# A hybrid decoder layer: loads, weight splits and row norms at the start of both feed-forward layers, rearranged

## The chip, the cores and the metric

The kernel runs on one core of a Trainium2 chip. The metric is the device time in microseconds of one execution, the median of the runs shown. TensorE multiplies matrices, VectorE and ScalarE work on elements, POOL (GpSimd) does further element work, and SP issues the transfers (DMA). Every engine has a queue of its own and takes its instructions in order; semaphores order the engines among each other.

## The reference

One layer for 64 sample rows and 1,024 prompt rows (T = 1,088 columns, with 1,024 features in KT = 8 tiles of 128 partitions). The parts around the change:

```python
def rmsnorm(x, g):
    y = xf * lax.rsqrt(jnp.mean(xf * xf, axis=-1, keepdims=True) + EPS)
    return (y * g).astype(x.dtype)
def swiglu(x, w_gate, w_up, w_down):
    return (jax.nn.silu(x @ w_gate) * (x @ w_up)) @ w_down
x = x + 0.5 * swiglu(rmsnorm(x, p['g_ffn1']), p['w1_gate'], p['w1_up'], p['w1_down'])
...                                   # mixer, output projection, cross attention
x = x + 0.5 * swiglu(rmsnorm(x, p['g_ffn2']), p['w2_gate'], p['w2_up'], p['w2_down'])
```

The hidden width is 2,816, 22 tiles of 128.

## The kernel before

Every matrix product of fp32 operands is made of three products of a rounded high part and a rest, the low part (L807 hi x hi, L808 lo x hi, L809 hi x lo). ScalarE or POOL writes high parts by a copy to fp32r, VectorE or POOL low parts by a subtraction. The 1,088 columns stand in three chunks, CH = 288, 512 and 288 columns.

A feed-forward layer has an opening and a steady part. The opening (`conventional` on TensorE, `ffn_layer` on ScalarE and VectorE) computes the first two hidden tiles in the plain way: gate 0 and up 0 for each chunk, then gate 1 for the three chunks, then up 1. The weights of tile 0 are split by POOL (`split_first`), those of tile 1 by ScalarE and VectorE (`conv_hi`, `conv_lo`). The gain g multiplies x before these products (it is part of the high and low parts), and the factor 1/rms of each column, `rstd`, multiplies the gate result (`gate_first`), before SiLU, and the up result (`ffn_up`).

The norm: the squares of x are added over the eight tiles to `acc` (128 partitions x 1,088). A product of `acc` with a 128x128 matrix of ones (`sum_chunk`, L835) puts the column sum of each chunk in all partitions; VectorE scales it to `rstd` (`mean_squares`, L1960), ScalarE takes the root (`rms`, L1460), VectorE the reciprocal (`inverse_rms`, L1968), each on 128 partitions x the chunk. The final norm of the kernel does it in another way: `acc` is the stationary operand and one column of ones the moving one (L985), so the sums stand as columns of 96 or 128 partitions; root (L1922) and reciprocal (L2749) work on these few columns, and a product with the identity (L998) spreads them to a row in all partitions.

The steady part computes the other twenty hidden tiles in quads, a block scheme with seven products in place of eight (`quad`; products 1 to 7 are j = 0 to 6 there, 24 matmuls x 2 of 272 columns each). It needs x times the gain (`gained`, L1497, ScalarE in place), sums and differences of quarter blocks of x (`moving_sum`, L2029, VectorE, four of them), and their high and low parts (`moving_hi`, L1501, ScalarE; `moving_lo`, L2037, VectorE), and the same of the weights (`quad_hi`, L1513; `quad_lo`, L2058). VectorE takes results out (`quad_part`, L2085; C11, C22, C21 and C12 are its four blocks), `keep_p1` (L1528, ScalarE) and `keep_u2` (L2106, VectorE) keep intermediate ones. In TensorE's `quad`, product 3 waits for `keep_p1`, product 5 for `keep_u2` and product 7 for the eviction of C22.

The order within each engine's queue is written out by hand. In the first opening ScalarE's queue is: high parts of x, high part of the gate 1 weights, 24 squares, three roots, high part of up 1, then for each chunk two tiles of `gained` and the SiLU of the chunk, two more tiles of `gained`, high parts of the block sums. VectorE's: low parts of x, sums of squares with the gate results of tile 0 copied out between, low part of gate 1, three `mean_squares`, for each chunk reciprocal and `gate_first`, low part of up 1, `ffn_up` of chunk 0, the first block sums (they wait for four `gained` tiles), `ffn_up` of chunk 1, the second and third block sums (they wait for all eight), `ffn_up` of chunk 2, and the operands of the first quad. In the second opening the squares are made in the projection before it.

Of the kernel before, what the change touches and what calls it, by code (L numbers as in the profile page):

```python
# [22 lines left out]
F32 = mybir.dt.float32  # L23
F32R = mybir.dt.float32r
ALU = mybir.AluOpType
# [96 lines left out]

SUM_BANK, RSTD_BANK, LAST_BANKS = 5, 2, DOWN_BANKS[:6]
# [70 lines left out]
def build(nc, t_in, t_out):  # L194
    ctx = ExitStack()
    with ctx:
# [32 lines left out]
        small = at("small", [P, NSM], C0 + 1440)  # L229

# [165 lines left out]
        x_in = [sem(f"x_in{c}") for c in range(NC)]  # L396
        ones_set = sem("ones_set")
# [9 lines left out]
        F_TOTAL = dict(gu_in=32, gu1_in=32, raw_in0=16 * (FI - 1), raw_in1=16 * (FI - 1), cv_a=4, cv_hi=2, cv_lo=2,  # L407
# [79 lines left out]

        y_done, y_tab, eps_set, row_mm = sem("y_done"), sem("y_tab"), sem("eps_set"), sem("row_mm")
# [14 lines left out]
        def _(sp):  # L503
            def load_first(f, w, m, done):
                for i in range(2):
                    sp.dma_start(raw_gu[i][:, m, :, :], w[i, :, m, :, :]).then_inc(f[done], 16)
# [176 lines left out]
            load_first(f, t_in["w_gu2"], 0, "gu_in")  # L683
            load_first(f, t_in["w_gu2"], 1, "gu1_in")
# [15 lines left out]
        def _(pool):  # L700
# [10 lines left out]
            def split_first(f):  # L711

                one = ones[:, :].unsqueeze(1).to_broadcast([P, KT, P])
                pool.wait_ge(f["gu_in"], upto(f, "gu_in", 32))
                steps = Steps(pool, f["cv_a"], upto(f, "cv_a", 0))
                for i, k in enumerate(("gate0", "up0")):
                    steps.done(pool.tensor_tensor(c_hi[k][:, :, :], raw_gu[i][:, 0, :, :], one, ALU.mult))
                    steps.done(pool.tensor_tensor(c_lo[k][:, :, :], raw_gu[i][:, 0, :, :],
                                                  c_hi[k][:, :, :].bitcast(F32), ALU.subtract))
# [81 lines left out]
        def _(pe):  # L801
# [35 lines left out]

            def conv_gate(f, t, c, feed=None):
# [11 lines left out]
            def conventional(f, feed, before, after):  # L850
# [10 lines left out]
                for c in range(NC):  # L861
                    conv_gate(f, 1, c)
# [2032 lines left out]
```

## Time and profile before

| | us |
|---|---|
| median of 3 runs | 2226.09 (2224.31 to 2226.76) |
| the profiled execution, its own time | 2230.03 |
| its span, first to last instruction | 2228.1 |
| TensorE busy | 2166.5 |
| VectorE busy | 1345.7 |
| ScalarE busy | 712.0 |
| POOL busy | 399.7 |

The busy times are those of one profiled execution; matmuls overlap, and a busy TensorE is not one at its peak. The granted clock of TensorE has two levels, 1.0 (2.4 GHz) and 0.5 (1.2 GHz), and was 0.991 on average. The first feed-forward opening lies at the start of the span, to about 103 us, the second from about 1462 to 1547 us.

### The profile page before, as it was taken

The numbers are of one execution on the slowest core, as the hardware profiler recorded it, in microseconds if no ns is written. First come the engines' busy times: TensorE is split into PE (matmuls) and PEld (weight loads), VectorE is DVE, ScalarE is ACT, GpSimd is POOL, SyncE is SP. The second block draws the span as 40 slices with busy tenths as digits, with TensorE's granted clock in tenths as the row PEclk, the third lists the DMA queues.
The fourth block names the chain that finished last, engine by engine and source line by source line (L and its number), as shares of the span: only waits on it lengthen the run. The fifth ranks groups of instructions, "written<-read, shape, count | busy, mean of one in ns | idle before, by whom it ended". The sixth has DMA issues, their size and how long they took to land. (4 is left out here: it accounts for less than half of the span.)

```text
span 2228.1 us, 37795 instructions
## 1 busy us (share of the span) xinstructions
PE 2166.5 (97%) x15020; PEld 2016.9 (91%) x15020; DVE 1345.7 (60%) x2013; ACT 712.0 (32%) x1270; POOL 399.7 (18%) x427
## 2 busy tenths in 40 slices
PE   6899999999999999989999999999999999999998
PEld 5899999998989888878898887989999999989897
DVE  7966766664423678899526155368766766644234
ACT  6422322322212325547403034154223223222122
POOL 1000000000000256768535321520000000000003
PEclk9999999999999999999999999999999999999999
DMA  3212212116423221153411062312122122164222
GB/s 139 77 59 96 76 58 96 67 59 236 125 67 93 73 96 39 59 143 103 163 38 58 20 246 77 135 40 78 59 96 76 58 96 76 59 232 125 66 72 81
DMA packets 70864, 206.67 MB, mean 93 GB/s; under 512 B 9703, under 2 KB 31207, under 8 KB 63079
## 3 DMA queue, kind: packets, MB, share of 16 engines
q1 hardware_dynamic: 67808, 201.84, 26.7%
q10 hardware_dynamic: 2951, 3.35, 0.4%
q8 instruction: 76, 1.25, 0.2%
q14 instruction: 29, 0.24, 0.0%
HBM read 161.14 MB, written 41.23 MB: 91 GB/s over the span
## 5 line engine op out<-in xcount | busy, mean ns | idle before, releaser
L807 PE MATMUL ps<-act_hi,op_hi 128*128 128x272 f32 x1280 | 370.2, 289 | 10.2 <-ACT p L1528 9.6
L808 PE MATMUL ps<-act_lo,op_hi 128*128 128x272 f32 x1280 | 371.6, 290 | 0.0
L809 PE MATMUL ps<-act_hi,op_lo 128*128 128x272 f32 x1280 | 370.8, 290 | 0.0
L707 POOL TENSOR_TENSOR w_hi<-w_raw,ones 128x256 fp32r<-128x256 f32 x148 | 134.4, 908 | 1033.3 <-DMA w_raw<-in_w_plain 790.6
L807 PE MATMUL ps<-act_hi,w_hi 128*128 128x288 f32 (+1 forms) x864 | 290.4, 336 | 7.3 <-DVE act_lo L1981 2.0
L807 PE MATMUL ps<-hs_hi,dn_hi 128*128 128x288 f32 (+1 forms) x864 | 284.9, 330 | 1.3 <-DVE x L2161 1.1
L809 PE MATMUL ps<-act_hi,w_lo 128*128 128x288 f32 (+1 forms) x864 | 283.9, 329 | 0.0
L808 PE MATMUL ps<-hs_lo,dn_hi 128*128 128x288 f32 (+1 forms) x864 | 282.4, 327 | 0.0
L809 PE MATMUL ps<-hs_hi,dn_lo 128*128 128x288 f32 (+1 forms) x864 | 282.3, 327 | 0.0
L807 PE MATMUL ps<-t_hi,op_hi 128*128 128x272 f32 x960 | 277.2, 289 | 0.2 <-DVE hid_t L2002 0.2
L808 PE MATMUL ps<-t_lo,op_hi 128*128 128x272 f32 x960 | 277.1, 289 | 0.0
L809 PE MATMUL ps<-t_hi,op_lo 128*128 128x272 f32 x960 | 277.1, 289 | 0.0
L808 PE MATMUL ps<-act_lo,w_hi 128*128 128x288 f32 (+1 forms) x792 | 259.6, 328 | 0.0
L807 PEld LDWEIGHTS ps<-act_hi,op_hi 128*128 128x128 f32 x1280 | 243.3, 190 | 11.1 <-issue 10.5
L808 PEld LDWEIGHTS ps<-act_lo,op_hi 128*128 128x128 f32 x1280 | 243.0, 190 | 0.0
L809 PEld LDWEIGHTS ps<-act_hi,op_lo 128*128 128x128 f32 x1280 | 243.0, 190 | 0.0
L1513 ACT ACTIVATE op_hi<-sums 128x512 fp32r<-128x512 f32 x160 | 101.2, 632 | 382.6 <-DVE sums L2066 208.2
L807 PEld LDWEIGHTS ps<-act_hi,w_hi 128*128 128x128 f32 x864 | 162.8, 188 | 25.7 <-issue 8.0
L807 PEld LDWEIGHTS ps<-t_hi,op_hi 128*128 128x128 f32 x960 | 181.2, 189 | 0.4 <-issue 0.4
L809 PEld LDWEIGHTS ps<-t_hi,op_lo 128*128 128x128 f32 x960 | 181.2, 189 | 0.0
L808 PEld LDWEIGHTS ps<-t_lo,op_hi 128*128 128x128 f32 x960 | 180.7, 188 | 0.0
L807 PEld LDWEIGHTS ps<-hs_hi,dn_hi 128*128 128x128 f32 x864 | 162.0, 188 | 17.9 <-DVE x L2161 3.4
(332 smaller groups left out, 4215.1 us busy)
## 6 DMA issues: line engine op xcount, KB each, us to landing
raw_gu<-in_w_gu SPq DMA_DIRECT2D x40, 1024.0 KB, 5.1
w_raw<-in_w_plain SPq DMA_DIRECT2D x54, 512.0 KB, 3.6
dn_raw<-in_w_dn SPq DMA_DIRECT2D x44, 512.0 KB, 4.2
hid<-hid_o SPq DMA_DIRECT2D x40, 544.0 KB, 3.7
hr<-hid SPq DMA_DIRECT2D x88, 144.0 KB, 2.1
hr<-hid SPq DMA_DIRECT2D x44, 256.0 KB, 2.7
x<-x_keep SPq DMA_DIRECT2D x16, 544.0 KB, 5.1
ck_T<-in_ck SPq DMA_DIRECT2D x8, 1024.0 KB, 7.2
```

Of the source, the lines that this page charges most:

```text
L707: steps.done(pool.tensor_tensor(hi[:, r, :], raw[:, r, :], one, ALU.mult))
L807: pe.matmul(out, wh, ah, start=(first and n == 0), stop=False, skip_group_check=goes_on)
L808: pe.matmul(out, wh, al, start=False, stop=False, skip_group_check=goes_on)
L809: ins = pe.matmul(out, wl, ah, start=False, stop=end, skip_group_check=goes_on)
L1513: act.activation(op_hi[j][:, :, :], src, ACT.Copy).then_inc(f["w_hi"], 1)
```

## The change

It rearranges both openings. Loads: in the first opening the gate 0 weights come ahead of x, x's first chunk is loaded in two halves, the up 0 weights behind it. An activation on one element right after the constants loads ScalarE's table; ScalarE makes the high part of gate 0 there, and POOL splits in pieces of two tiles of 128 columns (SHORT = 2). Norms: `sum_chunk`, `mean_squares`, `rms` and `inverse_rms` give way to `sum_columns`, `roots`, `inverse_columns`, `row` and `take_row`, in the way of the final norm, in both openings. Order: `normed(1)` and `normed(2)` (the wait for a row and `gate_first`) stand behind the first block sums and behind `ffn_up` of chunk 1; `keep_p1` stands ahead of operands 5 and 6 (j = 4 and 5) on ScalarE; the fourth block sums stand behind `keep_u2` on VectorE, and operand 6 (j = 5) ahead of the low parts of these sums. The identity is loaded once more for each opening. The core of the diff:

```diff
+COL_BANK, ROW_BANKS = 6, (7, 6, 7)
+        n_id = at("n_id", [P, P], C0 + 1440)
 # sync
+            load_first(f, t_in["w_gu1"], 0, 0, "gt_in")
             for c, (o, n) in enumerate(CH):
                 if c == 0:
-                    load_first(f, t_in["w_gu1"], 0, "gu_in")
-                sp.dma_start(x[:, :, o:o + n], t_in["x"][:, :, o:o + n]).then_inc(x_in[c], 16)
-            load_first(f, t_in["w_gu1"], 1, "gu1_in")
+                    sp.dma_start(x[:, 0:KH, o:o + n], t_in["x"][:, 0:KH, o:o + n]).then_inc(x_half_in, 16)
+                    sp.dma_start(x[:, KH:KT, o:o + n], t_in["x"][:, KH:KT, o:o + n]).then_inc(x_in[c], 16)
+                    load_first(f, t_in["w_gu1"], 1, 0, "gu_in")
+                else:
+                    sp.dma_start(x[:, :, o:o + n], t_in["x"][:, :, o:o + n]).then_inc(x_in[c], 16)
+            for i in range(2):
+                load_first(f, t_in["w_gu1"], i, 1, "gu1_in")
+            sp.dma_start(n_id[:, :], t_in["ident"]).then_inc(n_tab, 16)
 # gpsimd, split_first: pieces of SHORT tiles; the high part of the first gate 0 is left to ScalarE
+                        for r in rows:
+                            ins = pool.tensor_tensor(c_hi[k][:, r, :], raw_gu[i][:, 0, r, :], one, ALU.mult)
 # tensor
+            def sum_columns(key, c, adds):
+                w, at_ = WIDTH[c], CH[c][0]
+                pe.wait_ge(sq_used, SQ0[key] + adds)
+                if c and key == "ffn1":
+                    pe.wait_ge(rms_done, SUM0[key] + c)
+                for k in range(COLUMNS[c]):
+                    i = sum(COLUMNS[:c]) + k
+                    ins = pe.matmul(ps[0:w, COL_BANK, i:i + 1], acc[:, at_ + k * w:at_ + (k + 1) * w], ones[:, 0:1],
+                                    start=True, stop=True)
+                ins.then_inc(ssq_mm, 1)
+            def row(f, key, c):
+                w = WIDTH[c]
+                pe.wait_ge(rstd_done, SUM0[key] + c + 1)
...
+                for k in range(COLUMNS[c]):
+                    ins = pe.matmul(ps[:, ROW_BANKS[c], k * w:(k + 1) * w],
+                                    rms_col[c][0:w, k:k + 1].to_broadcast([w, P]), n_id[0:w, 0:w],
+                                    start=True, stop=True)
+                ins.then_inc(row_mm, 1)
+            def norm_ffn1(i):          # i = 0..2 behind up 0 of chunk i, 3..5 behind gate 1 of chunk i - 3
+                if i == 1:
+                    sum_columns("ffn1", 0, KT)
+                if i == 2:
+                    row(ffn["ffn1"], "ffn1", 0)
+                    sum_columns("ffn1", 1, 2 * KT)
+                if i == NC:
+                    sum_columns("ffn1", 2, 3 * KT)
+                if i > NC:
+                    row(ffn["ffn1"], "ffn1", i - NC)
+            def norm_ffn2(i):
+                if i == 0:
+                    for c in range(NC):
+                        sum_columns("ffn2", c, 2 * KT)
+                if i == 1:
+                    row(ffn["ffn2"], "ffn2", 0)
+                    row(ffn["ffn2"], "ffn2", 1)
+                if i == 2:
+                    row(ffn["ffn2"], "ffn2", 2)
 # scalar
+            def roots(key, which):
+                for c in which:
+                    w, k, i = WIDTH[c], COLUMNS[c], sum(COLUMNS[:c])
+                    act.wait_ge(ssq_mm, SUM0[key] + (c + 1 if key == "ffn1" else NC))
+                    act.activation(rms_col[c][0:w, 0:k], ps[0:w, COL_BANK, i:i + k], ACT.Sqrt, bias=eps[0:w, :],
+                                   scale=1.0 / D).then_inc(rms_done, 1)
+            def take_row(f, key, c):
+                o, n = CH[c]
+                act.wait_ge(row_mm, f["n"] * NC + c + 1)
+                act.activation(rstd[:, o:o + n], ps[:, ROW_BANKS[c], 0:n], ACT.Copy).then_inc(ssq_ev, 1)
                 conv_hi(f, "up1")
+                if key == "ffn1":
+                    roots(key, [2])
+                else:
+                    take_row(f, key, 0)
+                    take_row(f, key, 1)
                 for c in range(NC):
                     gained(f, gain, range(2 * c, 2 * c + 2))
+                    if c and (c == 2 or key == "ffn1"):
+                        take_row(f, key, c)
                     silu(f, 0, c)
                 gained(f, gain, range(2 * NC, KT))
...
+                keep_p1(f, Quad(0))
                 for j in range(4, 6):
                     quad_hi(f, Quad(0), 0, j)
-                keep_p1(f, Quad(0))
...
+            act.activation(act_hi[:, 0, 0:1], c_("g_ffn1", 0), ACT.Copy, scale=c_("g_ffn1", 0)).then_inc(table_set, 1)
+            act.wait_ge(ffn["ffn1"]["gt_in"], 16)
+            act.activation(c_hi["gate0"][:, :, :], raw_gu[0][:, 0, :, :], ACT.Copy).then_inc(ffn["ffn1"]["cv_a"], 1)
...
-            for c in range(NC):
-                chunk_squares(c)
-            rms("ffn1")
+            chunk_squares(0)
+            chunk_squares(1)
+            roots("ffn1", [0])
+            chunk_squares(2)
+            take_row(ffn["ffn1"], "ffn1", 0)
+            roots("ffn1", [1])
 # vector
+            def inverse_columns(key, which):
+                for c in which:
+                    w, k = WIDTH[c], COLUMNS[c]
+                    dve.wait_ge(rms_done, SUM0[key] + c + 1)
+                    dve.reciprocal(rms_col[c][0:w, 0:k], rms_col[c][0:w, 0:k]).then_inc(rstd_done, 1)
             def ffn_layer(f, key):
-                for c in range(NC):
-                    inverse_rms(key, then=lambda c: gate_first(f, c), which=[c])
+                def normed(c):
+                    dve.wait_ge(ssq_ev, SUM0[key] + c + 1)
+                    gate_first(f, c)
+                normed(0)
                 conv_lo(f, "up1")
+                if key == "ffn1":
+                    inverse_columns(key, [2])
                 ffn_up(f, 0, 0)
                 dve.wait_ge(f["xg"], upto(f, "xg", KH))
                 moving_sum(f, 0, 0, 0, TH, 0, 0)
+                normed(1)
                 ffn_up(f, 0, 1)
+                normed(2)
                 dve.wait_ge(f["xg"], upto(f, "xg", KT))
...
+                moving_lo(f, 4, lambda a: act_hi[:, a:a + 2, TH:T], lambda a: act_lo[:, a:a + 2, TH:T], 0, TH)
+                quad_lo(f, Quad(0), 0, 4)
+                keep_u2(f, Quad(0))
                 dve.wait_ge(f["t_sum"], upto(f, "t_sum", 6))
                 moving_sum(f, 0, 0, KH, 0, KH, TH)
-                moving_lo(f, 4, ...)
-                quad_lo(f, Quad(0), 0, 4)
-                keep_u2(f, Quad(0))
+                quad_lo(f, Quad(0), 0, 5)
                 dve.wait_ge(f["t_sum"], upto(f, "t_sum", 8))
                 moving_lo(f, 6, lambda a: t4_hi[:, a:a + 2, :], lambda a: t4_lo[:, a:a + 2, :], 0, 0)
-                quad_lo(f, Quad(0), 0, 5)
-            mean_squares("ffn1", D, which=[0, 1])
-            mean_squares("ffn1", D, which=[2])
+            inverse_columns("ffn1", [1])
```

## Rows read from the trace of the kernel before

**Rows 1.** The page's part 1: busy us (share of the span) xinstructions of each engine.

```profile
PE 2166.5 (97%) x15020; PEld 2016.9 (91%) x15020; DVE 1345.7 (60%) x2013; ACT 712.0 (32%) x1270; POOL 399.7 (18%) x427
```

**Rows 2.** TensorE's list of waits, 0 to 110 us: us in total, times, longest.

```profile
PE ps L807 <- ACT p L1528: 6.1, 1, 6.1
```

**Rows 3.** TensorE's list of waits, 1460 to 1560 us.

```profile
PE ps L807 <- ACT p L1528: 3.6, 1, 3.6
...
PE ps L807 <- DVE sg L2085: 0.3, 1, 0.3
```

**Rows 4.** The chain of waits in the second opening: start us, us, what.

```profile
1488.96 0.48 PE ps L835 x2
...
1493.05 1.96 DVE rstd L1968
...
1495.40 3.36 DVE rstd L1968
...
1507.47 4.89 DVE x L2029 x4
...
1543.36 0.74 DVE sg L2085
```

**Rows 5.** TensorE's timeline in the first opening: start us, us, instruction.

```profile
47.55 0.29 PE L808 MATMUL ps<-act_lo,c_hi_gate 128*128 128x288 f32 x1
47.68 0.29 PE L809 MATMUL ps<-act_hi,c_lo_gate 128*128 128x288 f32 x1
...
99.54 0.36 PE L807 MATMUL ps<-act_hi,op_hi 128*128 128x272 f32 x1
```

**Rows 6.** Timeline of ScalarE, POOL and VectorE at the start; in brackets idle before, releaser.

```profile
11.08 1.28 ACT L1469 ACT_TABLE_LOAD   x1 [11.08 <-DMA x<-in_x]
...
12.82 2.35 POOL L717 TENSOR_TENSOR c_hi_up<-raw_gu,ones 128x1024 fp32r<-128x1024 f32 x1
...
13.01 16.32 DVE L1981 SCALAR_TENSOR_TENSOR act_lo<-x,cst,act_hi 128x288 fp32r<-128x288 f32 x24 [12.00 <-ACT act_hi L1469]
```

**Rows 7.** VectorE's timeline in the first opening.

```profile
45.13 1.22 DVE L2023 TENSOR_TENSOR c_lo_gate<-raw_gu,c_hi_gate 128x1024 fp32r<-128x1024 f32 x1
...
54.10 0.69 DVE L2017 TENSOR_TENSOR gate_t<-gate_t,rstd 128x512 f32<-128x512 f32 x1
...
59.06 2.48 DVE L2029 TENSOR_TENSOR x<-x 128x1088 f32<-128x1088 f32 x2
...
62.79 4.89 DVE L2029 TENSOR_TENSOR x<-x 128x1088 f32<-128x1088 f32 x4
```

**Rows 8.** ScalarE's timeline in the first opening.

```profile
49.41 2.28 ACT L1497 ACTIVATE x<-x,cst 128x1088 f32<-128x1088 f32 x2
...
55.55 0.62 ACT L1487 ACTIVATE gate_t<-gate_t 128x512 f32<-128x512 f32 x1
...
85.22 2.11 ACT L1501 ACTIVATE t_hi<-x 128x1088 fp32r<-128x1088 f32 x2 [0.74 <-DVE x L2029]
...
91.26 0.63 ACT L1513 ACTIVATE op_hi<-sums 128x512 fp32r<-128x512 f32 x1 [3.92 <-DVE t_lo L2037]
```

**Rows 9.** ScalarE's timeline in the second opening.

```profile
1491.27 2.28 ACT L1497 ACTIVATE x<-x,cst 128x1088 f32<-128x1088 f32 x2
```

**Rows 10.** TensorE by line and shape in the final norm: xcount, us in all, mean ns, idle.

```profile
L998 PE MATMUL ps<-y_id,lrup 128*128 128x128 f32 x8 | 1.1, 275 | 0.0
L985 PE MATMUL ps<-ones,acc 128*128 128x1 f32 x8 | 0.9, 239 | 0.0
```

**Rows 11.** Instructions of lines 1922 and 2749: duration ns min/median/max, first and last start.

```profile
L1922 ACT ACTIVATE lrup<-ps,lrup x3: 246/258/259, 2188.7 to 2218.5; 96x3 f32<-96x3 f32 x2, 128x4 f32<-128x4 f32 x1
...
L2749 DVE RECIPROCAL lrup<-lrup x3: 160/172/178, 2189.0 to 2220.1; 96x3 f32<-96x3 f32 x2, 128x4 f32<-128x4 f32 x1
```

**Rows 12.** Stretches of 2 us: busy us of each engine, granted clock, DMA share, GB/s.

```profile
80.00:82.00 2.00, 0.00 (x0) 0.00 (x0) 1.97 (x4) 0.00 (x0) 0.00 (x0) 0.63 0.00 0
...
90.00:92.00 2.00, 2.00 (x15) 2.00 (x15) 1.90 (x4) 0.74 (x2) 0.00 (x0) 0.81 0.00 0
```

More of the change, by code:

```diff
@@ L229, in build @@
         small = at("small", [P, NSM], C0 + 1440)
+        assert P <= 144
+        n_id = at("n_id", [P, P], C0 + 1440)
         ACC0 = P0 + 68608
@@ L503, in _, with load_first @@
         def _(sp):
-            def load_first(f, w, m, done):
-                for i in range(2):
-                    sp.dma_start(raw_gu[i][:, m, :, :], w[i, :, m, :, :]).then_inc(f[done], 16)
+            def load_first(f, w, i, m, done):
+                sp.dma_start(raw_gu[i][:, m, :, :], w[i, :, m, :, :]).then_inc(f[done], 16)
             def load_quad(f, w, q, s):
@@ L682, in _ @@
             sp.wait_ge(stored, 16 * 9)
-            load_first(f, t_in["w_gu2"], 0, "gu_in")
-            load_first(f, t_in["w_gu2"], 1, "gu1_in")
+            sp.dma_start(n_id[:, :], t_in["ident"]).then_inc(n_tab, 16)
+            load_first(f, t_in["w_gu2"], 0, 0, "gt_in")
+            load_first(f, t_in["w_gu2"], 1, 0, "gu_in")
+            for i in range(2):
+                load_first(f, t_in["w_gu2"], i, 1, "gu1_in")
             for m in range(KT):
@@ L711, in split_first @@
             def split_first(f):
-                one = ones[:, :].unsqueeze(1).to_broadcast([P, KT, P])
-                pool.wait_ge(f["gu_in"], upto(f, "gu_in", 32))
+                one = ones[:, :].unsqueeze(1).to_broadcast([P, SHORT, P])
                 steps = Steps(pool, f["cv_a"], upto(f, "cv_a", 0))
[L716 to L719, printed above, removed]
+                for i, (k, loaded) in enumerate((("gate0", "gt_in"), ("up0", "gu_in"))):
+                    pool.wait_ge(f[loaded], upto(f, loaded, 16))
+                    rows = [slice(r, r + SHORT) for r in range(0, KT, SHORT)]
+                    if f["n"] == 0 and k == "gate0":
+                        steps.n = 1
+                        pool.wait_ge(f["cv_a"], 1)
+                    else:
+                        for r in rows:
+                            ins = pool.tensor_tensor(c_hi[k][:, r, :], raw_gu[i][:, 0, r, :], one, ALU.mult)
+                        steps.done(ins)
+                    for r in rows:
+                        ins = pool.tensor_tensor(c_lo[k][:, r, :], raw_gu[i][:, 0, r, :],
+                                                 c_hi[k][:, r, :].bitcast(F32), ALU.subtract)
+                    steps.done(ins)
             def split_plain(s, p, hi=w_hi, lo=w_lo, less=0, both=True):
@@ L862, in conventional @@
                     conv_gate(f, 1, c)
+                    after(NC + c)
                 pe.wait_ge(f["cv_lo"], upto(f, "cv_lo", 2))
@@ L1913, in _ @@
             conv_hi(ffn["ffn2"], "gate1")
-            rms("ffn2")
+            roots("ffn2", range(NC))
             act.wait_ge(act_lo_done, SPLIT0["ffn2"] + NC * KT)
-            ffn_layer(ffn["ffn2"], "g_ffn2", 16 + 16 * KT)
+            ffn_layer(ffn["ffn2"], "ffn2", "g_ffn2", 16 + 16 * KT)
             def final_sqrt(c):
                 w, k = WIDTH[c], COLUMNS[c]
-                act.wait_ge(eps_set, 1)
+                act.wait_ge(eps_set, 2)
                 act.wait_ge(ssq_mm, SUM0["final"] + c + 1)
@@ L2275, in _ @@
             dve.memset(ones[:, :], 1.0).then_inc(ones_set, 1)
+            dve.memset(eps, EPS).then_inc(eps_set, 1)
             dve.wait_ge(cst_in, 16)
@@ L2729, in _ @@
             lo_parts("co", lambda k: xq[:, k, :])
-            plain_residual("co", PAIR_CO, "ffn2", "g_ffn2", lambda s: None,
-                           lambda: mean_squares("ffn2", D, which=[0, 1]))
-            mean_squares("ffn2", D, which=[2])
+            plain_residual("co", PAIR_CO, "ffn2", "g_ffn2", lambda s: None, lambda: None)
             conv_lo(ffn["ffn2"], "gate1")
+            inverse_columns("ffn2", range(NC))
             for c in range(NC):
```

39 lines of the change are left out of this document (24 added, 15 removed).

## The prediction

> **What bounds the kernel now.** Part 1 of the page comes first: TensorE is busy in 97% of the span, so a change of order can only win from its few idle places [rows 1]. The list of TensorE's waits gives those of the two feed-forward openings: 6.1 us in the first and 3.6 us in the second for `p`, the copy of the first block product (it releases the third of the seven products of the first quad) and, in the second, 0.3 us for `sg` [rows 2, 3]. The 0.3 us is the row that matters. `sg` at L2085 is VectorE's second eviction (C22), for which the seventh product waits. In the second opening that product begins as soon as this eviction ends, 1543.36 + 0.74 = 1544.1, start 1544.23. In the first it begins at 99.54 [rows 5]; VectorE's queue there ends the same eviction at 99.4. So the seventh product starts when VectorE lets it, and the waits for `p` before it cost nothing: what TensorE would save there it would wait for `sg` later. The chain of waits says so for the second opening: TensorE up to the third sum at 1488.96, then VectorE from the reciprocals at 1493.05 to `sg` [rows 4]. After the seventh product TensorE has no wait of note until the down products, so a shift of its start is the change of the time.
>
> **What goes.** Three reciprocals of whole rows (1.96, 3.36 and 1.96 us [rows 4]) and three takes of sums leave VectorE; on 96 or 128 columns a root costs 0.26 us and a reciprocal 0.17 [rows 11]. What comes instead is work on TensorE (columns and rows, 0.11 us each by [rows 10]: about 0.5 us + 0.7 us for a chunk of 288, 0.9 + 0.9 for the one of 512, against 1.8 us for the three old sums, so some 2 us more in each layer) and three takes on ScalarE. That TensorE work is hidden while `sg` decides; without that cover it would cost 2 us twice.
>
> **What VectorE waits for next.** It needs the scaled x (`gained`, ScalarE) before its second block sums, which began at 62.79 and 1507.47 [rows 7, 4]. Before, ScalarE scaled all eight tiles without waiting for VectorE's first block sums: from 49.41, the first opening needed 13.4 us to 62.79, the second 16.2 from 1491.27 [rows 8, 9]. Now `normed(1)` stands behind the first block sums in VectorE's queue, SiLU of chunk 1 stands before tiles 4 and 5 in ScalarE's, and `take_row` 2 and `normed(2)` stand before the SiLU that holds tiles 6 and 7. The two engines take turns. Behind each waiting SiLU in ScalarE's queue stand the next scalings, and VectorE's second block sums wait for those. From the first scaling: unchanged 6.2 us to the end of tile 3 (two pairs of 2.28, a table load of 1.28, a SiLU [rows 8, 6]), then the first block sums 2.5 [rows 7], normed(1) 0.6, SiLU 0.6, a pair 2.2, take 0.4, normed(2) 0.45, SiLU 0.4, the last pair 2.2, and some eight hand-overs of 0.05 to 0.1: 15.9 us. Durations of the row takes are those of ScalarE's 288 and 512 column operations [rows 8].
>
> **When the first scaling starts.** *Second opening.* Columns in place of two sums, +0.4 on 1488.96; rows 0 and 1, 1.6; take of row 1, 0.7: 1491.7, against 1491.27. With 15.9 the second block sums start at 1507.6, +0.1. *First opening.* VectorE's 24 low parts ran from 13.01 to 29.33, two of them held behind POOL's long splits for about 2 us each [rows 6]. Half of x and an early table load let them start near 8.6, when x has landed to the half (x's first chunk landed at 11.08 as the third load after the constants; now it is half of it as the second). But the splits of POOL are now twelve pieces instead of four, each with about 0.6 us (a quarter of 2.35) in which a low part can stand, and ScalarE's last high part is bound by x's landing as before; I take an end at 26.4 (25.1 to 27.0), 2.9 earlier. A table load and a root now stand between the second and third chunk of squares, +1.0. So the low part of the next weights, before 45.13 + 1.22 [rows 7], ends at 44.4. Then on the new path: the first gate product, 24 steps of 0.133 = 3.2 [rows 5], columns of chunk 2 0.6, the root 0.26, three hand-overs: scaling starts at 48.8, 0.6 earlier than before, because `roots(2)` stands in front of it. With 15.9: 64.7, +1.9. Bounds: VectorE's end at 25.1 with no loss at the table load gives 46.5 and -0.4; TensorE late by its start at the lower clock gives up to +3.4.
>
> **The tail.** The fourth block sums move behind `keep_u2`. ScalarE's high parts of them (1.1 us a half [rows 8]) now lie open before VectorE's low parts, with one operand's low part of 0.7 as cover: +0.7. And ScalarE's operand 7 waits for those low parts (the 3.92 us wait of [rows 8] is that wait); operand 6, which filled VectorE meanwhile, is already done: +0.8. Together +1.5 in each opening. `keep_p1` one place earlier lets products 3 to 5 run sooner, which is worth nothing while `sg` decides. So `sg`, and with it the seventh product, shifts by +1.9 + 1.5 = +3.4 (1.1 to 4.9) and by +0.1 + 1.5 = +1.6 (1.2 to 2.1).
>
> **What costs nothing.** The identity's load stands behind the first opening's weights and ahead of the second's; row 0 stands behind 144 products of the first two weight blocks, 19 us and more at 0.133 [rows 5], and the next loads in SP's queue, the quads' weights, wait for the low parts at 44 as they did at 46 [rows 7]. POOL's sixteen pieces in the second opening stand under the last product of the stage before; they would have to take twice their time (0.6 us of work each, a quarter of 2.35 [rows 6]) to delay the first gate product, and what they held back would be VectorE's low parts, 0.6 us each. The final norm only counts its rows from another base.
>
> **The clock.** TensorE runs products 3 to 6 sooner and then stands still until `sg`: in the first opening product 6 can end near 97.0 and 7 starts near 102.9, in the second 1540.8 and 1545.8, so 5 to 6 us idle. In the trace the granted clock fell to 0.5 (the 1.2 GHz level) in the 6.1 us stop at product 3 and stayed there until 90.8, 6.1 us after the restart at 84.6 [rows 2, 12]. Before, that cost nothing, since `sg` came later. Now the lower level would fall on product 7 and those after it, where TensorE is the path. Bounds: 0 if the clock holds, 3.0 for a whole 6.1 us at half; I take 2.3, nearer to the row of a stop of this length, and less than all of it, since the lower level may begin before the restart.
>
> **The sum.** 3.4 + 2.3 + 1.6 + 2.3 = +9.6 us. The profiled execution took 2230.03 us around a span of 2228.1; +9.6 makes 2239.6. It stood 3.9 above the median of the runs, 2226.09, so the median should be 2235.7. What a measurement of this kernel can tell from no change is about 0.2%, 4.5 us.
>
> **Rivals.** *The clock holds.* Everything as above without 2.3 twice: 2231.1. For it: the idle time stands between products, and the level also depends on what ran before; against it the stop named. Half of this case lies over 0.2%. *VectorE's shorter queue decides.* If ScalarE's scalings come before VectorE needs them, VectorE's saved 7.3 + 1.4 us and its head start carry through: `sg` 11.0 - 1.5 = 9.5 us sooner in the first opening; in the second TensorE's own products, 3 us later by the new matmuls, allow 3.5 of it. About 2213, faster. It decides from the point where the second scaling pair ends before 55.6 and SiLU 1 no longer waits for normed(1). For it: VectorE is the chain in [rows 4] and the reciprocals are 7.3 us of it. Against it: the queue order, by which scaling waits three times for VectorE. The Trainium skill (Perfetto Trace Analysis, Optimizing Scalar/DVE Operations) says that with a saturated VectorE it may pay to give work to ScalarE. By that rule the time would come out as in this rival, 2213; the trace agrees on the saturation, and no run here yet shows the order of turns. *Nothing to be seen.* The first opening's head start is larger than I take (scaling from 46.5) and the clock costs little: +1.1 + 1.2 + about 1, 2229.
>
> **How the numbers follow.** Forecast with clock loss 0.57, all of it over 0.2% slower. Clock holds 0.13, divided evenly between slower and same. Nothing to be seen 0.12, same. Faster 0.18. That makes slower 0.64, same 0.18, faster 0.18. Likeliest 2235.7, its own range 2231 to 2239.2 (4.9 + 3.0 + 2.1 + 3.0 = 13.0 at the top). The range of 8 in 10 reaches down through the case of no change to 2224.5; below that lies most of the faster rival, above 2239.2 about 0.05.
>
> **What would show it.** Right: in TensorE's list of waits the waits for `p` are gone and waits of 4 to 6 us for `sg` L2085 stand in their place; ScalarE shows waits for VectorE's `gate_t` and takes between the scaling pairs; the second block sums start near 64.7 and 0 to 1 us late in the second opening; VectorE shows waits for ScalarE of 1 to 4 us; the granted clock is 0.5 around product 7. Wrong: VectorE reaches the second block sums before 62 and 1507, or product 7 starts before 99 and 1544; or the turns are as I say but the clock stays at 1.0.

## The result and the profile after

The changed kernel took 2240.40 us in the median of 6 runs (2233.41 to 2242.98), the kernel before 2226.43 (6 runs, 2224.31 to 2228.82): ratio 1.0058, 95% interval 1.0046 to 1.0070. Run again beside some of the experiments it took 2237.1 (6 runs), ratio 1.0047 (1.0030 to 1.0064). All twelve together have their median at 2239.05. So the change is slower, as forecast, by 14.0 us in the first six runs and 10.8 in the second six, where 9.6 were forecast; the first median lies 1.2 us above the range's upper end of 2239.2, the second inside the range. The profiled execution took 2242.98 us around a span of 2240.9, 12.8 more than the span before.

Part 1 of the profile's page says that TensorE stayed the engine that is busiest by far; its 13.7 us more than in [rows 1] are about the whole loss, though the change gives it only 68 more instructions:

```profile
PE 2180.2 (97%) x15088; PEld 2031.6 (91%) x15088; DVE 1331.4 (59%) x2008; ACT 714.4 (32%) x1278; POOL 403.1 (18%) x447
```

From TensorE's list of waits, first opening (0 to 140 us) and, behind the second dots, second opening (1460 to 1600 us): us in total, times, longest.

```profile
...
PE ps L829 <- DVE sg L2190: 3.4, 1, 3.4
PE ps L829 <- DVE c_lo_gate L2128: 3.3, 1, 3.3
PE ps L829 <- DVE t_lo L2142: 3.0, 1, 3.0
...
PE ps L829 <- DVE sg L2190: 4.9, 1, 4.9
PE ps L868 <- DVE acc L2050: 1.1, 1, 1.1
```

The waits for `p` of [rows 2, 3] are gone, and in each opening a wait for `sg`, VectorE's second eviction, stands where before there was 0.3 us or none. New is the 3.3 us wait for `c_lo_gate`, the low part of the second weight block. TensorE's timeline at both places (start us, us, instruction, in brackets idle before and releaser):

```profile
43.38 0.61 PE L829 MATMUL ps<-act_hi,c_hi_gate 128*128 128x288 f32 x1 [3.28 <-DVE c_lo_gate L2128]
43.78 0.44 PE L830 MATMUL ps<-act_lo,c_hi_gate 128*128 128x288 f32 x1
44.02 0.44 PE L831 MATMUL ps<-act_hi,c_lo_gate 128*128 128x288 f32 x1
...
95.57 0.36 PE L829 MATMUL ps<-t_hi,op_hi 128*128 128x272 f32 x1 [2.96 <-DVE t_lo L2142]
103.74 0.57 PE L829 MATMUL ps<-act_hi,op_hi 128*128 128x272 f32 x1 [3.40 <-DVE sg L2190]
...
1554.86 0.56 PE L829 MATMUL ps<-act_hi,op_hi 128*128 128x272 f32 x1 [4.92 <-DVE sg L2190]
```

The seventh product starts at 103.74 instead of 99.54 [rows 5], +4.2, and in the second opening at 1554.86 instead of 1544.23. The steps of the gate product lie 0.24 us apart (43.78, 44.02), not 0.133 as in [rows 5]. The stretches of 2 us say why (start and end, length, busy us of TensorE, its weight loads, VectorE, ScalarE and POOL, each with its number of instructions; granted clock; DMA share; GB/s):

```profile
42.00:44.00 2.00, 0.62 (x2) 0.63 (x3) 2.00 (x5) 0.34 (x1) 0.00 (x0) 0.50 0.00 0
44.00:46.00 2.00, 2.00 (x10) 2.00 (x10) 1.25 (x2) 0.00 (x0) 0.00 (x0) 0.50 0.82 229
...
104.00:106.00 2.00, 2.00 (x10) 2.00 (x10) 1.97 (x4) 0.98 (x2) 0.00 (x0) 0.50 0.00 0
...
1486.00:1488.00 2.00, 2.00 (x7) 1.61 (x7) 1.95 (x5) 1.98 (x4) 0.00 (x0) 0.50 0.05 12
...
1556.00:1558.00 2.00, 2.00 (x11) 2.00 (x11) 2.00 (x5) 1.82 (x3) 0.00 (x0) 0.50 0.00 0
```

At all four places the granted clock is 0.5, the 1.2 GHz level, just where TensorE has work that others wait for.

VectorE's timeline of the first opening, to be held against [rows 7]:

```profile
42.11 1.22 DVE L2128 TENSOR_TENSOR c_lo_gate<-raw_gu,c_hi_gate 128x1024 fp32r<-128x1024 f32 x1
...
50.05 0.17 DVE L2077 RECIPROCAL lrup<-lrup 96x3 f32<-96x3 f32 x1 [4.80 <-ACT lrup L1534]
54.07 0.46 DVE L2107 TENSOR_TENSOR hid_t<-ps,gate_t 128x288 f32<-128x288 f32 x1 [3.84 <-ACT gate_t L1568]
...
56.19 2.49 DVE L2134 TENSOR_TENSOR x<-x 128x1088 f32<-128x1088 f32 x2 [1.17 <-ACT x L1578]
...
62.46 0.46 DVE L2122 TENSOR_TENSOR gate_t<-gate_t,rstd 128x288 f32<-128x288 f32 x1 [1.00 <-ACT rstd L1541]
65.62 4.90 DVE L2134 TENSOR_TENSOR x<-x 128x1088 f32<-128x1088 f32 x4 [2.70 <-ACT x L1578]
```

And ScalarE's, against [rows 8]:

```profile
49.76 0.26 ACT L1534 ACTIVATE lrup<-ps,lrup 96x3 f32<-96x3 f32 x1 [7.42 <-PE ps L868]
49.92 2.29 ACT L1578 ACTIVATE x<-x,cst 128x1088 f32<-128x1088 f32 x2
...
59.32 0.63 ACT L1568 ACTIVATE gate_t<-gate_t 128x512 f32<-128x512 f32 x1 [2.43 <-DVE gate_t L2122]
59.85 2.28 ACT L1578 ACTIVATE x<-x,cst 128x1088 f32<-128x1088 f32 x2
...
62.95 0.44 ACT L1568 ACTIVATE gate_t<-gate_t 128x288 f32<-128x288 f32 x1 [0.53 <-DVE gate_t L2122]
63.30 2.29 ACT L1578 ACTIVATE x<-x,cst 128x1088 f32<-128x1088 f32 x2
```

This is the late start and the taking of turns: VectorE's low part comes 3.0 us sooner than before, then VectorE waits 4.80 us for the root of chunk 2 and 3.84, 1.17, 0.77 (not shown), 1.00 and 2.70 us for other work of ScalarE, 14.3 in all, and ScalarE 7.42 us for TensorE's column sums and 2.43 and 0.53 us for VectorE. Its first scaling starts at 49.92 (49.41 before), and VectorE's second block sums at 65.62 (62.79), 15.7 us behind it. In the second opening the place to count from is VectorE's last addition of squares, here first in the kernel before and then in the changed one:

```profile
1474.70 1.36 DVE L1952 TENSOR_TENSOR acc<-acc,sq 128x544 f32<-128x544 f32 x2 [0.78 <-DVE x L2616]
```

```profile
1482.57 1.36 DVE L2050 TENSOR_TENSOR acc<-acc,sq 128x544 f32<-128x544 f32 x2 [0.78 <-DVE x L2730]
...
1501.04 2.29 ACT L1578 ACTIVATE x<-x,cst 128x1088 f32<-128x1088 f32 x2
...
1516.74 4.90 DVE L2134 TENSOR_TENSOR x<-x 128x1088 f32<-128x1088 f32 x4 [2.70 <-ACT x L1578]
```

So the profiled kernel enters the second opening 7.9 us late, its block sums are 9.3 us late and its seventh product 10.6. The 12.8 us of span are then 4.2 to the seventh product, 3.7 more up to the second opening, 2.8 within it, and 2.1 behind its seventh product. In the profile of the second six runs (span 2238.6) the same four parts are 3.7, 0.3, 2.8 and 3.7: the parts within the openings come again, nearly, those between and behind them do not.

In the second opening the first scaling comes 18.5 us behind the last addition of squares (1482.57 to 1501.04), before 16.6 (1474.70 to 1491.27 [rows 9]). TensorE's products there, first before, from the first gate product of the second chunk to the old third sum, then in the changed kernel, column sums and rows:

```profile
1477.16 0.80 PE L807 MATMUL ps<-act_hi,c_hi_gate 128*128 128x512 f32 x1
...
1488.80 0.65 PE L835 MATMUL ps<-acc,ones 128*128 128x288 f32 x2
```

```profile
1483.98 2.20 PE L868 MATMUL ps<-ones,acc 128*96 128x1 f32 x20 [1.05 <-DVE acc L2050]
1486.05 0.78 PE L829 MATMUL ps<-act_hi,c_hi_gate 128*128 128x512 f32 x1
...
1498.79 1.72 PE L883 MATMUL ps<-n_id,lrup 96*128 96x96 f32 x14
```

The 48 products of that chunk took 12.7 us instead of 11.6, at first at the lower clock, and the twenty column products 2.1 instead of 1.3 for the three old sums (1476.12 to 1477.16 and 1488.80 to 1489.06).

### The profile page after: what moved, and what is told of

Same layout as the page of the kernel before. It is cut to its first block and busy times, and to the rows that moved or that the text cites. A ratio compares the mean times of both kernels' runs of the same rounds, so it can differ in the third digit from the quotient of the medians.

```text
span 2240.9 us, 37971 instructions
## 1 busy us (share of the span) xinstructions
PE 2180.2 (97%) x15088; PEld 2031.6 (91%) x15088; DVE 1331.4 (59%) x2008; ACT 714.4 (32%) x1278; POOL 403.1 (18%) x447
## 5 line engine op out<-in xcount | busy, mean ns | idle before, releaser
L829 PEld LDWEIGHTS ps<-act_hi,op_hi 128*128 128x128 f32 x1280 | 243.0, 190 | 10.5 <-issue 8.7
L829 PEld LDWEIGHTS ps<-hs_hi,dn_hi 128*128 128x128 f32 x864 | 162.0, 188 | 18.6 <-DVE x L2266 3.5
```

Source lines behind the costliest of these rows:

```text
L829: pe.matmul(out, wh, ah, start=(first and n == 0), stop=False, skip_group_check=goes_on)
```

## The experiments

Medians are in us, each beside the kernel before on the same chip (2226.2 to 2227.2). The fourth and fifth columns are from the one profiled execution of each, which can lie some us above the median (loads_alone: 5.5): start of the seventh product in the first opening, and its distance from VectorE's second block sums. "Lower clock" is the mean over the runs of span times (1 - mean granted clock), the time that the lower level can have cost TensorE at most. It also counts the lower level where TensorE waits or is not the path: in the profile before, 17.1 us at that level (80.5 to 90.8 and 1527.8 to 1534.6) end before the seventh products, whose start VectorE sets.

| kernel | median | ratio (95%) | 7th product | distance | lower clock |
|---|---|---|---|---|---|
| before (beside the first four) | 2226.21 | 1 | 99.54 | 36.75 | 18.0 |
| changed | 2240.40 | 1.0058 (1.0046-1.0070) | 103.74 | 38.12 | 24.6 |
| changed, again | 2237.10 | 1.0047 (1.0030-1.0064) | 103.25 | 38.10 | 23.1 |
| tail_back | 2233.15 | 1.0030 (1.0019-1.0041) | 99.90 | 36.77 | 21.8 |
| columns_sooner | 2237.83 | 1.0048 (1.0034-1.0062) | 101.47 | 38.12 | 25.0 |
| no_turns | 2235.79 | 1.0039 (1.0026-1.0052) | 100.92 | 41.78 | 23.7 |
| product_twice | 2231.38 | 1.0021 (1.0012-1.0030) | 102.93 | 38.10 | 18.6 |
| loads_alone | 2222.44 | 0.9984 (0.9976-0.9993) | 96.31 | 36.77 | 20.0 |
| columns_alone | 2237.83 | 1.0046 (1.0031-1.0061) | 103.46 | 36.76 | 21.0 |
| copy_alone | 2228.98 | 1.0006 (0.9997-1.0014) | 99.01 | 36.78 | 18.0 |
| tail_alone | 2234.64 | 1.0031 (1.0018-1.0044) | 100.46 | 38.10 | 20.3 |
| woven | 2221.41 | 0.9982 (0.9973-0.9991) | 92.31 | 36.77 | 18.8 |
| woven_filled | 2220.31 | 0.9967 (0.9957-0.9978) | 92.47 | 36.79 | 18.3 |

The theory: the loss is a later seventh product, by the turns and by the tail, and the lower clock behind it. The rivals: the turns or the tail are hidden by VectorE's own work; or it is the loads; or the clock falls where it likes and the stops have nothing to do with it.

**The changed kernel again,** as it was:

> The changed kernel once more, as the measure for the others of this call. If the median of 2240.4 us is the kernel's own, it comes again within 1.5 us. If part of it was where the clock happened to fall in the stages between the two openings (24 us at the lower level in the changed kernel's profile against 17 us before), it comes out near 2237 and the profile shows 17 us there.

It came out at 2237.1, as in the second case, and its profile has 17 us at the lower level between the openings, not 24. Half of that difference is 3.4 us, about what the median fell by. That the one made the other is not shown: the two sets of six runs overlap (2233.41 to 2242.98 and 2233.71 to 2244.05), and the execution with 17 us itself took 2240.54.

**The tail back** (changed kernel, VectorE's queue):

```diff
+ moving_sum(f, 0, 0, KH, 0, KH, TH)      # with its two waits
  moving_lo(f, 4, ...); quad_lo(f, Quad(0), 0, 4); keep_u2(f, Quad(0))
- moving_sum(f, 0, 0, KH, 0, KH, TH)
- quad_lo(f, Quad(0), 0, 5)
  moving_lo(f, 6, ...)
+ quad_lo(f, Quad(0), 0, 5)
```

> The changed kernel with VectorE's tail in the order of before (fourth block sums ahead of the low parts of the fourth operand, low part 5 behind those of t4); everything else as changed. If the tail costs what the prediction said (1.5 us an opening), the distance from VectorE's second block sums to the start of the seventh product goes back from 38.1 us (103.74 - 65.62 and 1554.86 - 1516.74) to 36.75 as before (99.54 - 62.79), and the median from 2240.4 to about 2237.5. Rival: the new order of the tail is hidden, and the loss is the turns and the clock alone: both distances stay at 38.1 and the median at 2240.4.

The distance went back to 36.77 as expected, 1.35 us in each opening, but the median fell by 5.9 us from the twelve runs' 2239.05 (3.8 to 6.2 by the ratios), not by 2.9. TensorE's stops show where more can come from. In the changed kernel it stopped for `t_lo` and again for `sg`, and the clock was at 0.5 behind the second stop. Here (the seventh product, then stretches of 2 us) the clock fell in an earlier stop and was back before the seventh product:

```profile
99.90 0.36 PE L829 MATMUL ps<-act_hi,op_hi 128*128 128x272 f32 x1 [1.85 <-DVE sg L2190]
```

```profile
90.00:92.00 2.00, 2.00 (x11) 2.00 (x10) 2.00 (x3) 0.39 (x1) 0.00 (x0) 0.50 0.00 0
...
100.00:102.00 2.00, 2.00 (x17) 2.00 (x18) 1.97 (x4) 0.83 (x2) 0.00 (x0) 1.00 0.03 8
```

Part of the difference, 49.92 to 47.43 us at the first scaling, is not the tail's, which comes later: in this execution TensorE stopped only 0.5 us for the low part and kept its clock. In the second opening the clock fell behind the seventh product here too, for 3.4 us where the changed kernel had 6.8.

**The column sums sooner** (TensorE's queue, first norm):

```diff
  sum_columns("ffn1", 1, 2 * KT)
+ sum_columns("ffn1", 2, 3 * KT)
- if i == NC:
-     sum_columns("ffn1", 2, 3 * KT)
```

> The changed kernel with the column sums of chunk 2 of the first norm ahead of the second weight block's first gate product instead of behind it: they run in TensorE's stop from 40.0 to 43.4. By the reading that the scaling starts late because its queue holds the root of chunk 2, the first scaling goes from 49.92 to about 42.6 us. The second block sums then wait for the row of chunk 1, which stands behind the second gate product: from 65.6 to 60.6 if TensorE keeps its full clock there (63.2 if it falls as now), so 2 to 5 us off the median, 2235.4 to 2238. Rival: VectorE's own queue is the limit from 42 us on, and the scaling's start is worth nothing: second block sums stay at 65.6, median 2240.4.

ScalarE's timeline has the first scaling where it was expected, 7.6 us sooner, and the wait that takes its place:

```profile
42.34 2.28 ACT L1577 ACTIVATE x<-x,cst 128x1088 f32<-128x1088 f32 x2
...
55.70 0.60 ACT L1540 ACTIVATE rstd<-ps 128x512 f32<-128x512 f32 x1 [7.13 <-PE ps L883]
```

The next turn, the row of chunk 1, stands behind the second gate product, so the second block sums came at 63.35 and the seventh product 2.3 us sooner. The median is at the upper end of the expectation; against the changed kernel's second median (2237.1) it is no gain. The late start was real, but only one of a series of waits.

**Without the turns:**

```diff
  # ScalarE
- gained 0-1, silu 0, gained 2-3, take_row 1, silu 1, gained 4-5, take_row 2, silu 2, gained 6-7
+ gained 0-1, silu 0, gained 2-7, take_row 1, silu 1, take_row 2, silu 2
  # VectorE
- first block sums, normed(1), ffn_up 1, normed(2), second block sums, ffn_up 2
+ first block sums, second block sums, normed(1), normed(2), ffn_up 1, ffn_up 2
```

> The changed kernel with the turns taken out in both openings: ScalarE scales tiles 2 to 7 in one stretch behind the first SiLU, ahead of the row takes 1 and 2; VectorE makes its second block sums before it norms chunks 1 and 2. The turns theory: from the first scaling to the second block sums 10.8 us instead of 15.7 (three more pairs of 2.28 behind the SiLU), but the two products of chunks 1 and 2 then follow them, so that the third one ends 2.2 us sooner than 71.4; the seventh product starts 2.2 us sooner in each opening, median about 2236. Rival: the turns are hidden by VectorE's own work, its third product ends at 71.4 as now, median 2240.4.

ScalarE's six scalings run in one stretch, and the second block sums start 10.6 us behind the first scaling instead of 15.7:

```profile
52.44 6.67 ACT L1578 ACTIVATE x<-x,cst 128x1088 f32<-128x1088 f32 x6
```

Because the products of chunks 1 and 2 now follow, the distance grew by 3.7; together 1.4 us less an opening, not 2.2. The median, 2235.8, is 3.3 us under the twelve runs of the changed kernel. Its interval (1.0026 to 1.0052) overlaps those of the changed kernel, so that the turns cost time is shown by the 1.4 us in the trace, not by the median; it is less than a reading of the queues gave.

**The loads alone** (kernel before with the changed loads, POOL's short pieces and the first high part on ScalarE):

```diff
- load_first(f, t_in["w_gu1"], 0, "gu_in")          # gate and up, then x
+ load_first(f, t_in["w_gu1"], 0, 0, "gt_in")       # gate, half of x, the other half, up
...
- one = ones[:, :].unsqueeze(1).to_broadcast([P, KT, P])
+ one = ones[:, :].unsqueeze(1).to_broadcast([P, SHORT, P])
...
+ act.activation(c_hi["gate0"][:, :, :], raw_gu[0][:, 0, :, :], ACT.Copy)
```

> The kernel before with the loads in the order of need, POOL's splits in short pieces and the first high part on ScalarE, and nothing else of the change (old row sums, reciprocals, queue orders and tail). If VectorE's queue sets the start of the seventh product, its earlier end of the first low parts (29.3 to 25.6 us in the changed kernel) carries through: low part of the next weights from 45.13 to 42.1, seventh product from 99.5 to 96.5, median from 2226.4 to 2223.4. Rival: TensorE, which stops for 3 us before that low part and then runs at the lower clock, gives the head start back before the sums of the third chunk: 2226.4.

VectorE's low part of the next weights and TensorE's seventh product:

```profile
41.31 1.22 DVE L2046 TENSOR_TENSOR c_lo_gate<-raw_gu,c_hi_gate 128x1024 fp32r<-128x1024 f32 x1
```

```profile
96.31 0.36 PE L823 MATMUL ps<-act_hi,op_hi 128*128 128x272 f32 x1 [0.62 <-DVE sg L2108]
```

3.8 us sooner at the low part, 3.2 at the seventh product, 3.8 in the median: the head start goes through VectorE's chain, 3.2 of 3.8 us of it in this profile. This part of the change is good by itself.

**The columns alone** (changed kernel with loads, splits, copy and tail of before):

```diff
- load_first(f, t_in["w_gu1"], 0, 0, "gt_in")
+ load_first(f, t_in["w_gu1"], 0, "gu_in")
...
- one = ones[:, :].unsqueeze(1).to_broadcast([P, SHORT, P])
+ one = ones[:, :].unsqueeze(1).to_broadcast([P, KT, P])
...
- keep_p1(f, Quad(0))
  for j in range(4, 6):
      quad_hi(f, Quad(0), 0, j)
+ keep_p1(f, Quad(0))
...                                    # tail as in tail_back
```

> Both norms as columns as in the changed kernel, but loads, splits, copy and tail as before. The turns theory: with VectorE's low parts as late as before, the first scaling of the first opening starts 1.5 to 4 us later than 49.4 (by the clock under the gate product that the column sums stand behind) and the second block sums 15.7 us after it instead of 13.4; in the second opening they come 0.8 us later; the lower clock behind the seventh product costs 2 to 3 more. Sum +6 to +11: 2232 to 2237. Rival: the 7.3 us of reciprocals that leave VectorE pay by themselves, and what costs time in the changed kernel is the tail and the loads: below 2226.

2237.8, just above what was expected, 11.6 us over the kernel before. The first scaling starts at 50.99, the second block sums at 66.70, 15.7 us later. The seventh products come 3.9 us later in the first opening (103.46) and 3.0 in the second, counted from the last addition of squares (1480.47 to 1552.97, 72.5 us instead of 69.5), together 6.9; its profile, 8.4 us longer in span than the one before, does not show what makes the rest of the 11.6. That reciprocals of whole rows leave VectorE pays nothing here, with this order of the queues.

**The copy alone, and copy with tail** (kernel before; the second also has the changed tail, the reverse of the diff of tail_back):

```diff
+ keep_p1(f, Quad(0))
  for j in range(4, 6):
      quad_hi(f, Quad(0), 0, j)
- keep_p1(f, Quad(0))
```

> The kernel before with the copy of the first block product one place earlier in ScalarE's queue, ahead of high parts 4 and 5, and nothing else. By the reading that VectorE's second eviction sets the seventh product, the waits for the copy (6.1 and 3.6 us) go, products 3 to 6 run sooner, and the same time is waited for the second eviction: seventh product at 99.5 and 1544.2 as before, median 2226 if the clock holds there, up to 3 more where it falls behind that wait. Rival: the waits for the copy were real, and up to 6 us are gained: 2220.

> The kernel before with that earlier copy and VectorE's tail as in the changed kernel (fourth block sums behind the addition of u, low part 5 ahead of those of t4). The tail's price as seen in the changed kernel: 38.1 us from the second block sums to the seventh product instead of 36.75, so 1.35 us twice over the kernel with the copy alone, and the clock that falls behind the longer wait, 1.7 us for each 3.4 us: 2229 to 2233. Rival: the tail costs only behind the turns; here the distance stays at 36.75 and the time at 2226.

TensorE's waits in the first opening with the copy alone, then with copy and tail:

```profile
PE ps L807 <- DVE u L2106: 3.5, 1, 3.5
PE ps L807 <- DVE sg L2085: 2.8, 1, 2.8
```

```profile
PE ps L807 <- DVE sg L2085: 4.9, 1, 4.9
PE ps L807 <- DVE t_lo L2037: 3.0, 1, 3.0
```

The 6.1 us for `p` of [rows 2] became 3.5 and 2.8 us for VectorE, 6.3 in all, a little later, and the median is 1.8 us above before (ratio 1.0006, not told from 1). The tail's order then adds 5.7 us, more than expected (2234.6, not 2229 to 2233), 2.6 of it by the distance (36.78 to 38.10, twice). It is about the price found in the changed kernel (5.9), so it doesn't hang on the columns. How the other 3 us divide is open; the lower clock can have cost 2.3 more than with the copy alone.

**A product twice** (changed kernel, TensorE, first quad of each opening):

```diff
+ for again in range(2 if first and j == 5 else 1):
      for a in range(2):
          for k in range(KH):
              ins = three(...)
```

> The changed kernel in which the sixth product of the first quad of each opening is computed twice into the same bank (24 matmuls, 3.0 us at full clock), so that TensorE works on in the 3.4 and 4.9 us in which it waited for the second eviction; VectorE's queue is untouched. If the stop makes the clock fall, the 3.4 and 6.8 us at the lower level behind the seventh product go, which gives 1.7 and 3.4 us back: about 5 us under the unchanged one, 2235. Rival: the level behind the seventh product comes from what ran before the stop: it falls all the same and the extra product only delays the seventh one where it runs at the lower level, 2240 to 2242.

A product of the quad is 24 matmuls in all, not 24 twice: the sixth one of the kernel before runs from 96.49 to 99.38. The seventh product in the first opening, and stretches of 2 us behind it in both:

```profile
102.93 0.36 PE L829 MATMUL ps<-act_hi,op_hi 128*128 128x272 f32 x1 [0.37 <-DVE sg L2191]
```

```profile
104.00:106.00 2.00, 2.00 (x18) 2.00 (x17) 2.00 (x5) 1.79 (x3) 0.00 (x0) 1.00 0.00 0
...
1552.00:1554.00 2.00, 2.00 (x18) 2.00 (x17) 2.00 (x4) 1.32 (x3) 0.00 (x0) 1.00 0.01 4
```

The clock stays at 1.0, with 18 products in 2 us where the changed kernel had 10 and 11. The median is 5.7 us under that of the changed kernel run beside it (2237.1), with more work done and VectorE's queue as it was. This shows the clock's part of the loss, and that the stop brings it. The Trainium skill (TensorE: Matmul & The Clock Gate, HAM oscillation — how this bites in real kernels) tells of kernels whose idle stretches bring the lower clock; these rows agree.

**The parts woven.** The changed kernel with column sums sooner, tail back, rows sent as soon as they can be, and scalings ahead of what waits for VectorE:

```diff
  # TensorE, first opening: rows 1 and 2 behind the second block's first gate product
- if i > NC:
-     row(ffn["ffn1"], "ffn1", i - NC)
+ if i == NC:
+     row(ffn["ffn1"], "ffn1", 1); row(ffn["ffn1"], "ffn1", 2)
  # second opening: rows 0, 1 between gate and up product of chunk 1, row 2 of chunk 2
  # ScalarE
+ first:  gained 0-1, silu 0, gained 2-3, take_row 1, take_row 2, gained 4-5, silu 1, silu 2, gained 6-7
+ second: gained 0-3, take_row 0, take_row 1, silu 0, gained 4-5, silu 1, gained 6-7, take_row 2, silu 2
  # VectorE, first: normed(1), normed(2) behind the first block sums, ahead of ffn_up 1
  # second: normed(1) behind normed(0); gate_out 2 behind ffn_up 1; normed(2) behind the second block sums
```

> The changed kernel with the column sums of chunk 2 sooner, the tail of before, the rows sent as soon as their reciprocals are there (first opening: rows 1 and 2 behind the second block's first gate product; second: between a chunk's gate and up product), and the scalings ahead of what waits for VectorE; in the second opening VectorE takes the third gate product behind its first block sums. By the turns theory the first opening scales from 42.3 us, the second block sums start near 55.5 and the seventh product near 92.5 (99.5 before); in the second opening the block sums are about 12 us sooner than now, and TensorE's own products become the limit, 3 to 5 us sooner than before. Median 2211 to 2219. Rival: another wait takes over in the first opening (the copy of the first product, the low parts), and it comes out like the loads alone, 2222.

> The woven kernel with the sixth product of the first opening's first quad computed twice, as cover for the 3.7 us in which TensorE waits for the second eviction there. If the 6.8 us at the lower level behind that wait are what took the gain of the first opening back (7.2 us sooner at the seventh product), they go and the median falls by 3.4 us, from 2221.4 to 2218. Rival: the level falls anyway, or elsewhere, and it stays at 2221.

Woven: the second block sums, the seventh product, and a stretch behind it; then the same stretch with the product twice.

```profile
55.54 4.90 DVE L2149 TENSOR_TENSOR x<-x 128x1088 f32<-128x1088 f32 x4 [1.03 <-ACT x L1582]
```

```profile
92.31 0.57 PE L829 MATMUL ps<-act_hi,op_hi 128*128 128x272 f32 x1 [3.66 <-DVE sg L2205]
```

```profile
94.00:96.00 2.00, 2.00 (x11) 2.00 (x10) 1.99 (x4) 1.39 (x3) 0.00 (x0) 0.50 0.04 8
```

```profile
94.00:96.00 2.00, 2.00 (x18) 2.00 (x18) 2.00 (x4) 1.56 (x3) 0.00 (x0) 1.00 0.00 0
```

The first opening did what was expected (55.54, 92.31: 7.2 us sooner than before), yet the median of 2221.4 misses 2211 to 2219. The clock took about 3 of it back behind the 3.66 us stop (the lower level lasted from 91.6 to 98.4, and TensorE worked through 6.1 us of it), and from one seventh product to the other only 1.8 us less passed than before, since TensorE's own products leave little more in the second opening: it waits there for `sg` only 1.0 us. With the product twice the lower level is gone from that place; the median falls by 1.1 us and the ratio from 0.9982 to 0.9967, with intervals that overlap: the direction expected, the 3.4 us not shown. Woven_filled is the best version found, 0.33% (0.22 to 0.43) faster than the kernel before, the woven one and the loads alone 0.18 and 0.16%.

## Where the prediction was right, and which step of it failed

- *What bounds the kernel.* Right. In every kernel above TensorE's seventh product of the first opening starts where the second eviction ends. In the kernel before, the sixth product of the quad ends there too, so that profile alone could not tell; the copy alone could: the sixth product came sooner, the seventh waited 2.8 us for the eviction, and nothing was gained.
- *The turns.* Right in kind and size: 15.9 us were forecast from first scaling to second block sums, 15.7 came in both openings, before 13.4 and 16.2.
- *When the first scaling starts.* The step that failed, in both openings. First opening: the term "the first gate product, 24 steps of 0.133 = 3.2" measured 5.7 us (43.38 to 49.08), at the lower clock behind a stop of 3.3 us that the forecast did not have: with the loads sooner TensorE was done with the first block at 40.1, VectorE's low part at 43.3. Scaling began at 49.92, not 48.8, although the low part ended 1.1 us sooner than forecast (43.3 against 44.4): luck that hid part of the miss. In the second profile the stop was 1.8 us, the product took 4.8 (43.80 to 48.60), in part at the lower clock, and scaling began at 49.45. Second opening: the term "columns in place of two sums, +0.4" measured 1.9, counted from the last addition of squares: 0.8 for the column products themselves and 1.1 for the lower clock (0.5 from 1485.8 to 1489.2) under the products behind them, which the sum had put at nothing.
- *The tail.* Right: +1.5 forecast, +1.3 to +1.35 measured, in each opening and in two kernels.
- *So the seventh product.* +3.4 and +1.6 forecast, +4.2 and +2.8 measured (+3.7 and +2.8 in the second profile), within the bounds given for the first (4.9), above those for the second (2.1). The excess is that of the scaling's start.
- *The clock behind the seventh products.* Right in kind (product_twice) and in sum: 2.3 twice were forecast; the lower level lasted from the start of the product to 106.8 and to 1560.9, 3.1 and 6.0 us, of which half is 1.5 and 3.0, 4.5 together, and product_twice gave back 5.7. The stops in front were 3.4 and 4.9 us, not 5 to 6: in the first opening TensorE stood still another 3.0 us for `t_lo`, which the forecast did not have.
- *The sum.* The forecast against the two profiles, us more than before:

| part of the span | forecast | first | second |
|---|---|---|---|
| up to the first seventh product | 3.4 | 4.2 | 3.7 |
| from there to the last addition of squares ahead of the second opening | 2.3 | 3.7 | 0.3 |
| from there to the second seventh product | 1.6 | 2.8 | 2.8 |
| behind it | 2.3 | 2.1 | 3.7 |
| together | 9.6 | 12.8 | 10.5 |

The excess in the first and third row is the failed step. The second and fourth row change from one execution to the next; the lower clock between the openings (24 us at that level in the first profile, 17 in the second and before) is part of it, and no run says what sets it. By parts and medians: loads -3.8, columns with their order of queues +11.6, copy +1.8, tail +5.7, together +15.3, or +0.61% by ratios, against 0.58 and 0.47% for the whole.
- *The rivals.* "The clock holds" fell with the granted clock of 0.5 behind both seventh products. "VectorE's shorter queue decides" fell: its condition was a second scaling pair before 55.6 and a SiLU 1 that doesn't wait; the pair ended at 56.1 and the SiLU waited 2.43 us. It was to give 2213; the columns by themselves gave 2237.8. The Trainium skill (Perfetto Trace Analysis, Optimizing Scalar/DVE Operations) says that with a saturated VectorE it may pay to give work to ScalarE. VectorE was that before (busy in 44.3 of the 45 us from 45 to 90), yet columns_alone does not bear the rule out. Only with another order of the queues did the shorter work show, as 55.54 for the second block sums of the woven kernel. "Nothing to be seen" wanted the scaling from 46.5; it began at 49.92.

## What to carry to other kernels

Here, work taken off the engine that is the path paid only where what replaced it did not make that engine wait for a queue on another engine: follow each hand-over to the instructions that stand behind the waiting one. A wait of TensorE in front of a point that another engine's chain sets was no reserve: shortened in one place, it came back in another, and in the changed kernel it cost the clock behind it. When TensorE has to wait anyway, work on an operand that is there can cover the stop: a repeated product gave back 5.7 us in the changed kernel, and 1.1, not told from nothing, in the woven one.

## What the runs showed of the hardware

- The granted clock fell to 0.5 in stops of 3.3 us (at 42.0) and 4.9 us (at 1554.1), and the repeated product, which left stops of 0.4 and 1.9 us in front of the seventh products, kept it at 1.0 there.
- It also fell with no stop of that length: in the changed kernel, behind a wait of 1.1 us and 20 products of one column each, issued from 1483.98 to 1486.05, the stretch 1486 to 1488 is at 0.5. All eight other profiles with these column sums show a fall at the same point; in those of the kernels with the old sums (before, loads_alone, copy_alone, tail_alone) there is none. The wait does not make the difference: it was 1.6 us in columns_alone, where the clock fell, and 1.6 before and 1.2 in loads_alone, where it did not. What it is in these products that goes with the fall was not tested.
